# Taking the six modulation units of each layer between its first projections instead of in its tail, and the condition's SiLU and parameters first

## What is computed

```python
def first_block(x, ...):
    h = x
    for l in range(DEPTH):                       # DEPTH = 2
        h = h + hybrid_mixer(rmsnorm(h, norm_mix[l]), w_in[l], w_branch_a[l], w_branch_b[l],
                             b_gate[l], sink_logit[l], w_out[l])
        h = h + expert_choice_ffn(rmsnorm(h, norm_ffn[l]), w_router[l], w_expert_gate[l],
                                  w_expert_up[l], w_expert_down[l])
    return rmsnorm(h, norm_final)

def hybrid_mixer(h, w_in, w_branch_a, w_branch_b, b_gate, sink_logit, w_out):
    proj = jnp.einsum('bsd,dc->bsc', h, w_in)
    qa, ka, va, qw, kw, vw, gates = jnp.split(proj, SPLITS, axis=-1)
...
    g = jax.nn.sigmoid((gates + b_gate).astype(jnp.float32)).astype(h.dtype).reshape(B, S, N_BRANCH, D)
    merged = g[:, :, 0] * ya + g[:, :, 1] * yb
    return jnp.einsum('bsd,de->bse', merged, w_out)

def adaln(cvec, w, b):                           # w: 1024 x 6144
    m = jax.nn.silu(cvec) @ w + b
    return [t[..., None, :] for t in jnp.split(m, 6, axis=-1)]
```

## Time and profile before

| what | us |
|---|---|
| median of the 3 timed runs | 2413.95 |
| lowest and highest of them | 2413.58, 2418.01 |
| the profiled execution | 2417.26 |
| its span, first to last instruction | 2415.5 |
| of it, PE busy / DVE busy / ACT busy | 1740.8 / 665.8 / 546.2 |
| mean rate of the DMA over the span | 310 GB/s |

### The profile page before, as it was taken

How to read it: one execution, slowest core, us unless ns; L and a number is a source line. 1 busy time by engine, 2 the same in 40 slices (tenths; PEclk the granted TensorE clock), 3 DMA queues, 4 the chain that set the end, 5 groups by cost and what they waited for, 6 DMA issues and landing times.

```text
span 2415.5 us, 28680 instructions
## 1 busy us (share of the span) xinstructions
PE 1740.8 (72%) x12630; PEld 1058.1 (44%) x12630; DVE 665.8 (28%) x1059; ACT 546.2 (23%) x773; POOL 0.2 (0%) x4
## 2 busy tenths in 40 slices
PE   7999866565655989984677666689897655566654
PEld 7978712120212988850223232178787422222221
DVE  4486400000001558430331110075465300000001
ACT  4365200000001346410201211043443211111110
POOL 0000000000000000000000000000000000000000
PEclk9999987676877999997898888689899688888888
DMA  8425899999999631779999999943314499999995
GB/s 312 147 71 179 310 391 409 409 409 409 409 409 402 226 111 71 255 303 407 409 405 403 405 404 406 405 165 110 135 54 168 169 410 410 410 410 410 409 410 236
DMA packets 226730, 747.63 MB, mean 310 GB/s; under 512 B 5952, under 2 KB 18496, under 8 KB 226112
## 3 DMA queue, kind: packets, MB, share of 16 engines
q1 hardware_dynamic: 226624, 746.06, 79.5%
HBM read 744.99 MB, written 1.05 MB: 309 GB/s over the span
## 4 chain that ended last, share of the span: by engine, by line
DMA 44%; PE 40%; SPq 5%; DVE 5%; ACT 4%; issue 2%; DVEq 0%; ACTq 0%
PE bank L632 18%; DMA ring<-w_expert_down 14%; DMA ring<-w_expert_up 12%; DMA ring<-w_expert_gate 6%; DMA ring<-moe_w_up 6%; DMA ring<-moe_w_down 5%; SPq L2530 5%; PE bank L635 4%; PE bank L684 3%; PE bank L706 3%; PE bank L715 2%; PE bank L659 1%; PE bank L845 1%; PE bank L865 1%; PE bank L643 1%
## 5 line engine op out<-in xcount | busy, mean ns | idle before, releaser
L684 PE MATMUL bank<-ring,arena 128*32 128x512 f32 x3072 | 464.5, 742 | 314.7 <-DMA ring<-w_expert_up 137.6
L706 PE MATMUL bank<-ring,arena 128*32 128x512 f32 x1536 | 260.1, 814 | 191.5 <-DMA ring<-w_expert_down 119.9
L684 PEld LDWEIGHTS bank<-ring,arena 128*32 128x32 f32 x3072 | 97.2, 123 | 647.5 <-DMA ring<-w_expert_up 215.7
L632 PE MATMUL bank<-arena_parts,ring_parts 128*128 128x256 f32 x1376 | 317.6, 286 | 6.1 <-DVE ring_parts L2394 6.1
L632 PEld LDWEIGHTS bank<-arena_parts,ring_parts 128*128 128x128 f32 x1376 | 237.7, 193 | 15.0 <-DVE ring_parts L2394 6.3
L1336 ACT ACTIVATE arena<-bank 128x512 f32<-128x512 f32 (+1 forms) x162 | 91.8, 599 | 643.2 <-PE bank L696 463.6
L706 PEld LDWEIGHTS bank<-ring,arena 128*32 128x32 f32 x1536 | 49.5, 130 | 375.7 <-DMA ring<-w_expert_down 179.2
L1818 DVE TENSOR_TENSOR arena<-arena,bank 128x512 f32<-128x512 f32 x24 | 15.8, 685 | 689.3 <-PE bank L684 689.3
L632 PE MATMUL bank<-arena_parts 128*128 128x256 f32 x800 | 180.6, 283 | 15.8 <-DVE hnT_parts L1966 8.2
L632 PE MATMUL bank<-ring_parts 128*128 128x256 f32 x768 | 155.0, 292 | 15.3 <-DVE hnT_parts L2221 5.7
L632 PE MATMUL bank<-hnT_parts,ring_parts 128*128 128x256 f32 x544 | 155.8, 286 | 0.0
(11 more groups left out here) (320 smaller groups left out, 1969.9 us busy)
## 6 DMA issues: line engine op xcount, KB each, us to landing
ring<-w_expert_gate SPq DMA_DIRECT2D x64, 2048.0 KB, 23.6
ring<-w_expert_up SPq DMA_DIRECT2D x64, 2048.0 KB, 23.8
ring<-w_expert_down SPq DMA_DIRECT2D x64, 2048.0 KB, 23.9
ring<-w_in SPq DMA_DIRECT2D x34, 2048.0 KB, 8.8
ring<-moe_w_gate SPq DMA_DIRECT2D x32, 2048.0 KB, 23.6
ring<-moe_w_up SPq DMA_DIRECT2D x32, 2048.0 KB, 23.4
ring<-moe_w_down SPq DMA_DIRECT2D x32, 2048.0 KB, 23.7
ring<-ada_w SPq DMA_DIRECT2D x12, 2048.0 KB, 8.5
```

The lines of the kernel that those rows point to most:

```text
L632: last = pe.matmul(out[:, n * S:(n + 1) * S], w[:, k, n * P:(n + 1) * P], x[:, k, :], start=first, stop=final)
L684: last = pe.matmul(banks[bank0 + f][32 * e:32 * e + 32, :], x_slots[:, c, 32 * e:32 * e + 32], w[:, k, e, f * 512:(f + 1) * 512], start=c ...
L706: last = pe.matmul(banks[4 + d][32 * e:32 * e + 32, :], hidT[:, f, 32 * e:32 * e + 32], w[:, e, d * 512:(d + 1) * 512], start=f == 0, stop ...
```

## The change

The list of units of a layer is reordered (`HEAD_ORDER`): 0, 18, 1, 19, 2, 20, 3, 21, 4, 22, 5, 23, then 6 to 17. Everything that named a ring buffer by its unit now goes through the position (`HEAD_AT`); units 6 to 17 stand at positions 12 to 23, and so in the same buffers as before. PE takes modulation unit n right ahead of the first job that uses projection unit n. The banks are 7 (units 0 to 3) and 5 (units 4 and 5), and ACT copies them out behind jobs 6 and 10. The tail has none of it left. SP issues the six first expert units behind the last head unit, each after PE is through with one of units 12 to 17. In layer 0 the parameters are loaded ahead of x and the constants, and ACT applies SiLU ahead of the squares.

```diff
+HEAD_ORDER = [unit for n in range(ADA_UNITS) for unit in (n, 18 + n)] + list(range(ADA_UNITS, 18))
+HEAD_AT = {unit: p for p, unit in enumerate(HEAD_ORDER)}
...
+                def ada_unit(n):
+                    u = 18 + n
+                    if n % 4 == 0:
+                        ada_banks[n // 4] = take(7 - n // 2, "act", f"ada {min(n + 3, ADA_UNITS - 1)}")
+                    if layer == 0 and n == 0:
+                        pe.wait_ge(act_done, act_at("c_silu", loops))
+                    unit_ready(("head", u), layer)
...
                 for i in range(len(IN_JOBS)):
+                    unit = IN_JOBS[i][0]
+                    if unit < ADA_UNITS and (i == 0 or IN_JOBS[i - 1][0] != unit):
+                        ada_unit(unit)
                     job(i, hn_high, hn_low, hn_ready if i == 0 else None)
...
-                ada_bank = take(7, "act", "ada 3")
-                ada_unit(0)
-                ada_unit(1)
                 pe.wait_ge(dve_done, dve_at("merged low 3", loops))
...
-                sum_squares_part("norm2", squares, 2, norm_bank, "squares2")
-                ada_unit(2)
-                sum_squares_part("norm2", squares, 3, norm_bank, "squares2")
-                ada_unit(3)
+                for j in (2, 3):
+                    sum_squares_part("norm2", squares, j, norm_bank, "squares2")
...
-                ada_bank = take(7, "act", "ada 5")
-                ada_unit(4)
-                ada_unit(5)
                 pe.wait_ge(dve_done, dve_at("idx diag", loops))
...
-                pe.wait_ge(act_done, act_at("ada 5", loops))
...
+                else:
+                    act.wait_ge(params_loaded, 16)
+                    act.wait_ge(dve_done, dve_at("c_pad"))
+                    for r in range(2):
+                        act.activation(c_silu[:, :, r], par[:, Q_C + r * DC:Q_C + (r + 1) * DC], ACT.Silu)\
+                           .then_inc(act_done, act_p.mark("c_silu"))
+                    act.wait_ge(consts_loaded, 32)
...
+                    if i == 6:
+                        ada_copy(0, 4)
+                    elif i == 10:
+                        ada_copy(4, ADA_UNITS)
...
+            sp.dma_start(par[:], io["params"][0]).then_inc(params_loaded, 16)
             sp.dma_start(h3, io["xT"].rearrange("(c p) t -> p c t", p=P)).then_inc(consts_loaded, 16)
...
-                for i in range(UNITS1_HEAD):
+                for p, i in enumerate(HEAD_ORDER):
...
-                    if i == UNITS1_HEAD - 2:
-                        load_first(0)
-                        load_first(1)
-
-                    if i >= RING:
-                        sp.wait_ge(pe_done, pe_at(f"unit {i - RING}", loops))
+
+                    if p >= RING:
+                        sp.wait_ge(pe_done, pe_at(f"unit {HEAD_ORDER[p - RING]}", loops))
...
-                for u in range(2, RING):
-                    load_first(u)
+
+                for u in range(RING):
+                    sp.wait_ge(pe_done, pe_at(f"unit {HEAD_ORDER[UNITS1_HEAD - RING + u]}", loops))
+                    load_expert_unit(u, u, *experts, 0, FE)
```

More of the change, by code:

```diff
@@ L77 @@
 CTX_LOADS = {(1, 11): 0, (1, 18): 1, (1, 23): 2, (2, 6): 3, (2, 15): 4, (3, 1): 5}
+HEAD_ORDER = [unit for n in range(ADA_UNITS) for unit in (n, 18 + n)] + list(range(ADA_UNITS, 18))
+HEAD_AT = {unit: p for p, unit in enumerate(HEAD_ORDER)}
 def stream(layer):
-    units = [("head", i) for i in range(UNITS1_HEAD)]
+    units = [("head", i) for i in HEAD_ORDER]
     for t in range(TILES1):
@@ L921, in hn_ready @@
                         pe.wait_ge(dve_done, dve_at(f"hn1 low {k // 2}", loops))
+                ada_banks = {}
+                def ada_unit(n):
[5 more added lines that the diff above has]
+                    unit_ready(("head", u), layer)
+                    w = slot(HEAD_AT[u]).rearrange("p (k n) -> p k n", k=DC)
+                    for k in range(DC):
+                        for b in range(4):
+                            last = pe.matmul(ada_banks[n // 4][32 * b:32 * b + 32, (n % 4) * P:(n % 4 + 1) * P],
+                                             c_silu[:, k, :], w[:, k, b * P:(b + 1) * P], start=k == 0, stop=k == DC - 1)
+                    last.then_inc(pe_done, pe_p.mark(f"ada {n}", unit_done(u)))
                 for i in range(len(IN_JOBS)):
+                    unit = IN_JOBS[i][0]
+                    if unit < ADA_UNITS and (i == 0 or IN_JOBS[i - 1][0] != unit):
+                        ada_unit(unit)
                     job(i, hn_high, hn_low, hn_ready if i == 0 else None)
@@ L1482, in _, with ada_copy @@
                        .then_inc(act_done, act_p.mark(f"hn1 high {j}"))
[L1483 to L1488, removed]
+                def ada_copy(n0, n1):
+                    act.wait_ge(pe_done, pe_at(f"ada {n1 - 1}", loops))
+                    act.activation(ada_rows[:, (layer * ADA_UNITS + n0) * P:(layer * ADA_UNITS + n1) * P],
+                                   banks[7 - n0 // 2][:, 0:(n1 - n0) * P], ACT.Copy).then_inc(act_done, act_p.mark(f"ada {n1 - 1}"))
                 for i, (_, c0, step, _, reader) in enumerate(IN_JOBS):
@@ L1585, in _ @@
                 root("norm2", bank=banks[6])
[L1587 to L1592, removed]
                 act.wait_ge(dve_done, dve_at("router max", loops))
@@ L2583, in _ @@
                     elif layer:
-                        sp.wait_ge(pe_done, pe_at(f"tile_{TILES1 - 1} unit {UNITS1_TILE - RING + i}", loops, layer=1))
+                        sp.wait_ge(pe_done, pe_at(f"tile_{TILES1 - 1} unit {UNITS1_TILE - RING + p}", loops, layer=1))
                     if i < 12:
-                        load_cols(i, w_in, starts[i], 256 if i == 4 else 512)
+                        load_cols(p, w_in, starts[i], 256 if i == 4 else 512)
                     elif i < 14:
-                        load_cols(i, io["w_branch_a"][layer][(i - 12) * P:(i - 11) * P, :], 0, D)
+                        load_cols(p, io["w_branch_a"][layer][(i - 12) * P:(i - 11) * P, :], 0, D)
@@ L2589, in _ @@
                     elif i < 16:
[L2590 removed]
+                        load_cols(p, io["w_branch_b"][layer], 512 * (i - 14))
                     elif i < 18:
[L2592 removed]
+                        load_cols(p, io["w_out"][layer], 512 * (i - 16))
                     else:
[L2594 to L2596 removed]
+                        load_cols(p, io["ada_w_2"], 512 * (layer * ADA_UNITS + i - 18))
```

17 lines of the change are left out of this document (6 added, 11 removed).

## The result

The changed kernel is slower: 2437.66 us in the median of four runs (2435.27 to 2443.47) against 2414.89 for the kernel before (2413.58 to 2418.01, four runs), a ratio of 1.010 with a 95% interval of 1.0085 to 1.0115. That is +22.8 us; the forecast was +20, to 2434, with a range of 2426 to 2442. A second set of runs on another occasion gave 2439.99 against 2419.16, ratio 1.0096 (1.0072 to 1.0119); the two medians by themselves are 20.8 us apart. The profiled execution took 2436.34 us with a span of 2434.6, 19.1 longer than the span before.

What follows compares the result with a forecast made beforehand. PE bounds the gapless first projections, transfers the expert tiles. A layer: 9.4 + 0.1 - 1.9 + 2.9 - 0.3 = +10.2 us; two layers +20.4 on a 2413.95 median gave a forecast of 2434 us, range 2426 to 2442.

Steps and rivals of the forecast that it cites:

- The bound: First projections: PE has no gap, so each matmul put between two jobs lengthens the stage by its own duration.
- Units 1 to 5: +9.4 us a layer: First projections: modulation units 1 to 5 between gapless jobs, 5 x 1.88 us, all on the path.
- Unit 0 and the start: Ahead of the first job: unit 0 fits PE's wait in layer 1, costs 0.2 us (0 to 0.7) in layer 0.
- the term of -0.3 in the forecast: Before the first job: modulation unit 0 shortens PE's gap and the low clock there, 0.3 us less a layer.
- The tail gives back 1.9 us: Tail: only modulation unit 2 is on the path, saving 1.9 us a layer; the other five cover waits, saving 0.
- The clock: +2.9 us a layer between 0 and 5.1: Tail: three new PE gaps (`w_out` jobs, router, slot numbers) lower the clock behind them, costing 1.7, 0.8 and 0.4 us.
- the halfway value for the router: Router's 3.0 us gap in the tail: clock cost taken as 0.8 us, halfway between 0 and 1.7.
- The ring that is full sooner: 0: Before the expert tiles: expert loads issued earlier save 0, since the ring is already full and waits for PE.
- The tiles: Expert tiles: bound by transfers, they move as a block with their start; nothing in them changes.
- Starvation: Rival, first projections: late projection loads stall PE 18.7 us a layer, giving 2472 us; chance 5%.
- The tail that returns all six: Rival, tail: all 11.3 us of modulation units come back, -1.9 us a layer, giving 2410 us; chance 5%.
- the expert stream that starts earlier: Rival, expert tiles: earlier transfers gain 21 us a layer in full, giving 2371 us; chance 4%.

Runs made afterwards that it cites:

- thinned kernel: The changed kernel with 4 of the 32 matmuls of each modulation unit left, in the new places; 2913.35 us, not comparable with the full kernels' times.
- thinned old order: The kernel before with 4 of the 32 matmuls of each modulation unit left, in the old tail places; 2910.73 us, not comparable with the full kernels' times.
- the start alone: The kernel before with parameters loaded ahead of x and SiLU ahead of the squares, modulation units still in the tail; 2415.48 us against 2419.16, ratio 0.9989.
- three-and-three order: The kernel before with modulation unit 2 behind the last part of the sum of squares, 3 to 5 inside the top-k; 2408.17 us against 2417.11, ratio 0.9966.
- kernel with filled gaps: The changed kernel with useless matmuls, 2, 1 and 2 modulation units' worth, in the three new tail gaps; 2429.04 us, ratio 1.0049 to the kernel before.
- kernel with held loads: The changed kernel with expert units 2 to 5 of the first six issued late again; 2440.27 us against the changed kernel's 2439.99.

## Why the prediction was right, and where its terms were off

**The bound.** That PE has no gap in the projections and that a unit there costs its own length held: the thinned kernel got back 1.58 us per unit, with all loads in place. The two thinned kernels, old order and new, lie 2.6 us apart, the full ones 22.8 and 20.8.

**Units 1 to 5: +9.4 us a layer.** The step was right and its size too small; this is the term that was mis-sized most. I priced a unit from two that run back to back in the tail. Between jobs each also pays the 0.2 us at the change of kinds, so five cost 5 x 2.08 = 10.4, and two layers 2.0 us more than I had. With unit 0 the stage was forecast at +18.4 us for both layers and measured at +20.8.

**Unit 0 and the start.** In layer 1 the unit is free: from the norm's sum (780.40 before, 789.15 after) to the first job it is 8.3 us in both kernels. In layer 0 I took 0.2 and set the end at 0.7, on the ground that the same bytes stand ahead of unit 0. ACT begins with unit 0 at 13.38 instead of 12.74, and the start alone showed such a delay too, so this ground failed; the unit itself ran at half clock as expected (3.62 us in its window). The first job starts at 22.46 instead of 21.16, but only some 0.4 us of it remain at the end of the second. What gives the rest back is the term of -0.3 in the forecast: PE has been at work on unit 0, and from 22.5 to 24.5 the granted clock is 1.00, where it was 0.50 before. Taken from the lengths of the stage, that is worth some 0.9 us in layer 0 and 0.4 in layer 1.

**The tail gives back 1.9 us.** Held: the waits grew to 5.0, 3.0 and 6.7 us, the numbers of the forecast to the tenth, and the thinned old order showed that the other five units return nothing. The three-and-three order shows the same from the other side: the tail of layer 0 is 2.0 us shorter with unit 2 in a wait, without any unit leaving it.

**The clock: +2.9 us a layer between 0 and 5.1.** The tail grew by 1.6 and 1.4 us where 1.9 went out, so the clock took 3.5 and 3.3. I gave 1.7, 0.8 and 0.4 to the three gaps. (The equal waits ahead of the burst L965, which this rests on, do not stand in the earlier trace rows; the trace has 2.0 us in both layers.) In layer 0 they cost 1.35 (18.67 against 17.32), 1.5 (5.12 against 3.61) and 0.8 (the slot numbers, 2.07 against 1.23; the gather behind them took 5.4 in both). In layer 1 they cost 1.9 (19.14 against 17.23), 1.7 (5.30 against 3.61) and nothing (2.07 in both). So the halfway value for the router was the one that was too low: its 3.0 us of idle cost nearly the full price in both layers. In the second profile the clock took 3.4 and 2.2 us, so the forecast of 2.9 is right within what changes from one execution to the next. By the rule of the Trainium skill ("TensorE: Matmul & The Clock Gate", "Why this matters for your kernels") idle gaps between bursts of matmuls are to be avoided, because the clock falls back. The trace agrees for the gaps of 5.0 and 3.0 us. The one of 6.7 us cost 0.8 us and nothing, since the gather behind it was slow before the change too (5.43 and 5.71 us against 3.58 in a later tile). The kernel with filled gaps shows that it is the idle time that does it.

**The ring that is full sooner: 0.** Held, by the kernel with held loads, within the few us that its four runs can tell.

**The tiles.** I said that they only move as a block. In layer 0, 3.5 us of their length went away. From the first expert unit to PE's start on the last one it is 469.3 us instead of 470.6; PE ran at a clock of 0.50 for some 3 us of the first unit instead of 5.5, and the DMA took up work again about 1 us sooner after PE's start. The larger part is at the end, where the last products of the tile run on PE and no transfer is waited for, and their clock changed:

```profile
785.25 3.91 PE bank L719 x16
789.15 3.47 PE bank L647 x16
```

Before, this burst took longer:

```profile
774.45 5.95 PE bank L715 x16
```

That is 2.0 us less; in layer 1 the same burst went from 5.92 to 3.91. It is no gain of the change: in the second profile of the same kernel the burst of layer 0 is back at the old length:

```profile
785.90 5.86 PE bank L719 x16
791.76 3.47 PE bank L647 x16
```

And kernels with the old tail have the short one as well: 3.90 us in layer 0 of the thinned old order, 3.91 there in the three-and-three order, 3.90 in layer 1 with the start alone. Over the nine profiles the burst takes either 3.90 to 3.91 us or 5.48 to 5.95. The tiles of layer 0 take 476.8 to 478.0 us where it is short and 480.6 to 481.6 where it is long.

The burst behind the projections does the same in the opposite sense: 7.40 us before and 5.86 after in layer 0, 5.84 and 7.38 in layer 1. The burst at the end of the tiles stands behind a wait of 1.3 us, the one behind the projections behind some 4.4 us in which PE is mostly idle, and which of them meets the low clock changes from one execution to the next. The profiled executions differ by 19.1 us where the medians are 22.8 and 20.8 apart, and such bursts of 1.5 to 2 us each are enough for a difference of this size; which of them made it is open.

**How much of the total is luck.** By stages the forecast was +18.4 us for the projections, +2.0 for the tails and nothing elsewhere. The two profiles give +20.8 and +3.0 for these, and +1.4 for attention, -6.8 for the tiles and +0.6 for the second block. The steps were right; that their sum is so near +20.4 is in part because errors and clock effects of either sign made up for each other.

**The rivals.** Starvation: between the jobs PE waited for nothing; its only wait from 20 to 115 is 0.4 us for DVE. The tail that returns all six, and the expert stream that starts earlier: both out, by the thinned old order and, for the 21 us a layer that it stood for, by the held loads.

## What to carry to other kernels

Work that nothing waits for belongs where its engine waits for another one. Read the waits of that engine one by one, with their lengths, and fill each to just under its length; a stage in which the engine has no gap is the worst place, even if loads are hidden there best. Before moving work out of a wait, add the price of the clock that the new idle time costs to the bursts behind it. A load that comes sooner is worth something only if somebody is late for it: look at whether the DMA still works when the consumer arrives.

## What the runs showed of the hardware that I had not expected

- A group of matmuls with 32-column weight tiles and 128-column products, put between jobs with 128-column tiles and 256-column products, costs PE some 0.2 us beside its own matmuls, whether the group holds 4 matmuls or 32 (rounds of 11.87 and 13.39 us against 11.3 + 0.36 and 11.3 + 1.88).
- A wait of 3.0 us ahead of the router was enough for a lower clock in both layers (5.12 and 5.30 us instead of 3.61), and a wait of 1.2 us was not (3.61). At other places waits as short went either way: the burst at the end of the tiles took 3.91 or 5.95 us behind 1.3 us, the gather of the three-and-three order 5.44 us in layer 0 and 3.81 in layer 1 behind the same 1.3 us.
- One small load of 98 KB moved to the head of the queue, in front of x, delayed x by some 0.8 us and the first unit of the ring by some 0.5 in the mean of six profiles against three, though it had been in front of the ring's units before. Why is open.
- Five units' worth of matmuls of no use per layer, in three waits, made the changed kernel faster: 2429.04 us instead of 2437.66, and +11.9 instead of +22.8 us against the kernel before.
